# Two of five half swaps of the rotary step: from TensorE matmuls to copies within on-chip memory

## The chip, the cores and the metric

The kernel runs on one core of one Trainium2 chip. The metric is the device time of one execution in microseconds (us); lower is better. The kernel before was measured three times: 1043.47 us in the median, 1043.19 to 1046.55 over the three. On one core five engines work side by side, each on an instruction list of its own: TensorE (PE, matmuls; PEld is its weight load), VectorE (DVE), ScalarE (ACT), GpSimd (POOL) and SyncE (SP, which here only starts the weight transfers). They meet through counting semaphores.

## The reference

The reference is a trunk of two layers on 272 tokens (16 meta tokens and 256 frames) of width 1024. Each layer is a gated feed-forward, a token mixer and a second feed-forward, each between two RMS norms. Layer 0 mixes with stick-breaking attention, layer 1 with grouped-query attention in a sliding window (16 query heads, 4 key heads, head width 64). The change touches layer 1's rotary positions alone:

```python
def rope(t, pos):
    half = HEAD_DIM // 2
    ...
    t1, t2 = tf[..., :half], tf[..., half:]
    return jnp.concatenate([t1 * cos - t2 * sin, t2 * cos + t1 * sin], axis=-1)
```

So each head of queries and keys is its own value times cos, plus its two halves of 32 values swapped, times sin, with a minus on the first half. After it come the scores, the mask, the softmax with sinks, the product with the values and the output projection.

## The kernel before, in words

Activations are kept transposed: a 128-row tile holds two heads (64 rows each) and the tokens lie along the columns. Weights come from HBM in 156 panels of 128 x 2048 float32, 1 MB each. ScalarE rounds a panel half into `w_hi` (L517), VectorE writes what is left into `w_lo` (L765), and TensorE adds three products (w_lo y_hi, w_hi y_hi, w_hi y_lo: L1152 to L1154) for each float32 product. SP starts the load of the panel after next when VectorE has finished both halves of the one that lay in the same buffer (L463).

The attention of layer 1 is written out by hand as a pipeline of slots `st`, in which every engine does the same step of different head pairs. The input projection gives key rows (`b = 0`) and four panels of two query tiles (`b = 1` to `4`). In slot `st` TensorE does one projection tile (`in_tile(st)`, slots 0 to 5; 24 matmuls), then in slots 0, 2, 4, 6 `rotate(b)`, then `scores(st - 1)` (L1397), `values(st - 4)` (L1424), units of the output projection (`out_unit`, 12 matmuls each, from slot 6), and `turn(st - 3)`, which transposes the softmax weights (L1412).

`rotate(b)` (L1370 to L1383) swaps the halves: a float32 matmul of the constant 128 x 128 matrix `rot` with each of the two query tiles, into PSUM bank 5. The minus stands in `rot`. `rope(b)` on VectorE (L971) multiplies that by sin into `rot_s` (L976) and adds `rot_c` (L980), the product with cos, which GpSimd makes (L493). GpSimd does nothing else by then: its loop waits for the query tiles of panel `b` (`sw_drained` at 7 for b = 3, at 9 for b = 4), then makes `rot_c`.

VectorE's order in a slot is: `normalise(st - 3)` (L1002 to L1009), one half of `w_lo` (L765), `drain_tile(st)` (L968, which moves a query tile out of PSUM and raises `sw_drained`), `rope` in slots 2, 4, 6, then `logits(st - 1)` (L993), then `o_low(st - 4)` (L1014), which writes `sw_lo`, an operand of `out_unit`. `rope(3)` stands in slot 4 and `rope(4)` in slot 6; the tile that completes panel 3 is drained in slot 3, the one that completes panel 4 in slot 5. ScalarE's order is `save_p` (L658), a half of `w_hi` (L517), `exps` (L667, L670), then `o_high` (L675), which writes `sw_hi`.

`scores(p)` needs the rotated panel 2 + p//2 and the logits of the pair before; `out_unit(j, n)` needs `sw_lo` of pair 2j + 1.

Of the kernel before, what the change touches and what calls it, by code (L numbers as in the profile page):

```python
# [25 lines left out]
P = 128  # L26
D = 1024
KT = D // P
SEQ = 256
META = 16  # L30
L = META + SEQ
DEPTH = 2
FF = 2816
HD = 64
# [52 lines left out]
SW_K, SW_V, SW_Q = 0, 2, 4  # L87
# [114 lines left out]
def build(nc, first_in, x_in, gains_in, sinks_in, row_in, panels_in, const_in, out):  # L202
    ctx = ExitStack()
    with ctx:
# [3 lines left out]
        def sem(name):  # L208
            return ctx.enter_context(nc.semaphore(name))

        ps = ctx.enter_context(nc.psum_tensor("ps", [P, 8, 512], F32))
# [38 lines left out]
        with ExitStack() as over:  # L250
            first = over.enter_context(nc.sbuf_tensor("first", [P, KT * FIRST_K], F32))
        with ExitStack() as over:
            def mix_sb(name, shape, dt=F32):
                return over.enter_context(nc.sbuf_tensor(name, shape, dt))
            qkv = mix_sb("qkv", [P, 3 * KT, L])
# [8 lines left out]
        with ExitStack() as over:  # L264
            def swa_sb(name, shape, dt=F32):
                return over.enter_context(nc.sbuf_tensor(name, shape, dt))
            swa_sb("under_qkv", [P, 12, L])
            kx = swa_sb("kx", [P, 2, L])
            v_win = swa_sb("v_win", [P, 2, 4, P])
            vt = swa_sb("vt", [P, 4, NKV * HD])  # L270
            rot_s = swa_sb("rot_s", [P, 2, L])
            rot_c = swa_sb("rot_c", [P, 2, 2, L])
            s = swa_sb("s", [P, 3, 2, SW_W])
            p_t = swa_sb("p_t", [P, 2, 2, 512])
            sw_hi = swa_sb("sw_hi", [P, KT, SEQ], F32R)
            sw_lo = swa_sb("sw_lo", [P, KT, SEQ], F32R)
            neg_sinks = swa_sb("neg_sinks", [P, NH])
            neg = swa_sb("neg", [P, 3, 2, 2])
            tot = swa_sb("tot", [P, 3, 2, 2])
            snk = swa_sb("snk", [P, 3, 2, 2])  # L280
            den = swa_sb("den", [P, 3, 2, 2])
            inv = swa_sb("inv", [P, 3, 2, 2])
# [110 lines left out]
        oh_ready = sem("oh_ready")  # L393
        ol_ready = sem("ol_ready")
        rot_done = sem("rot_done")
        rs_ready = sem("rs_ready")
        rc_ready = sem("rc_ready")
        roped = sem("roped")
# [78 lines left out]
        @block.gpsimd  # L477
        def _(pool):

            nc.gpsimd.memset(post_ln[:], 0.0).then_inc(warm_zero, 1)  # L480

            pool.wait_ge(tile_drained, 1)
            for r in range(2):
                nc.gpsimd.memset(w[:, r, :, 0:SB_PAD], 0.0).then_inc(pad_zero, 1)
            pool.wait_ge(const_in_sem, 16)
            for b, at in enumerate((1, 3, 5, 7, 9)):
                pool.wait_ge(sw_drained, at)
                if b >= 2:

                    pool.wait_ge(roped, b - 1)  # L490
                row = SW_K if b == 0 else SW_Q + 2 * b - 2
                c0 = 0 if b == 0 else META
                nc.gpsimd.tensor_tensor(rot_c[:, b % 2, :, c0:L], qkv[:, row:row + 2, c0:L],  # L493
                                        spread(cst("cos"), 2, c0), ALU.mult).then_inc(rc_ready, 1)
                if b == 1:
                    for n, (c, k0, zero) in enumerate(SW_WIN):
                        if zero:
                            nc.gpsimd.memset(v_win[:, :, n, 0:zero], 0.0).then_inc(win_ready, 1)
                        tokens = SW_TOKENS[c][k0 + zero:k0 + P]
                        cut = [i for i in range(len(tokens)) if i == 0 or tokens[i] != tokens[i - 1] + 1] + [len(tokens)]  # L500
                        for i0, i1 in zip(cut, cut[1:]):
                            nc.gpsimd.tensor_copy(v_win[:, :, n, zero + i0:zero + i1],
                                                  qkv[:, SW_V:SW_V + 2, tokens[i0]:tokens[i0] + i1 - i0])\
                                .then_inc(win_ready, 1)
# [254 lines left out]
        def _(v):  # L759
# [68 lines left out]
            for t in SUBS:  # L828
# [121 lines left out]
                elif t.kind == "swa":  # L950
# [20 lines left out]
                    def rope(b):  # L971
                        c0 = 0 if b == 0 else META
                        row = SW_K if b == 0 else SW_Q + 2 * b - 2
                        turned = ps[:, 0:2, 0:L] if b == 0 else ps[:, 5, :].rearrange("p (a n) -> p a n", a=2)
                        v.wait_ge(rot_done, b + 1)
                        nc.vector.tensor_tensor(rot_s[:, :, c0:L], turned, spread(cst("sin"), 2, c0),  # L976
                                                ALU.mult).then_inc(rs_ready, 1)
                        v.wait_ge(rs_ready, b + 1)
                        v.wait_ge(rc_ready, b + 1)
                        nc.vector.tensor_tensor(qkv[:, row:row + 2, c0:L], rot_s[:, :, c0:L],  # L980
                                                rot_c[:, b % 2, :, c0:L], ALU.add).then_inc(roped, 1)
                        v.wait_ge(roped, b + 1)
# [165 lines left out]
        def _(pe):  # L1148
# [8 lines left out]
            for t in SUBS:  # L1157
# [197 lines left out]
                elif t.kind == "swa":  # L1355
# [83 lines left out]
                    def out_unit(j, n):  # L1439

                        g = t.g_out + j
                        pe.wait_ge(lo_ready, 2 * g + 2)
                        pe.wait_ge(ol_ready, 8 + 2 * j + 2)
                        if j == 0 and n < 2:
                            pe.wait_ge(sw_drained, 8 + n)
                        elif j == 0 and n == 2:
                            pe.wait_ge(rs_ready, 5)
                        elif j == 0:
                            pe.wait_ge(neg_ready, 4 * PAIRS)
                        for d in (2 * n, 2 * n + 1):  # L1450
                            for c in range(2):
                                opens = j == c == 0 and (d % 2 == 0 or n == 3)
                                mm = three(out_tile(ps, t, d), g % SLOTS, D * c + P * d, sw_hi[:, 2 * j + c, :],
                                           sw_lo[:, 2 * j + c, :], opens, j == 3 and c == 1, shared=n < 3)
                            if j == 3:
                                mm.then_inc(f_done, 1)
                        if j < 3 and n == 3:
                            mm.then_inc(panel_done, 1)

                    pe.wait_ge(const_in_sem, 16)  # L1460
                    for st in range(SW_SLOTS):
                        if st < SW_TILES:
                            in_tile(st)
                        for unit in SW_FILL.get(st, ([], []))[0]:
                            out_unit(*unit)
                        if st == 0:
                            rotate(0)
                            rotate(1)
                        elif st in (2, 4, 6):
                            rotate(st // 2 + 1)  # L1470
                        if 0 <= st - 1 < PAIRS:
                            scores(st - 1)
                        if st == 1:
                            turn_v()
                        if 0 <= st - 4 < PAIRS:
                            values(st - 4)
                        for unit in SW_FILL.get(st, ([], []))[1]:
                            out_unit(*unit)
                        if 0 <= st - 3 < PAIRS:
                            turn(st - 3)  # L1480
# [106 lines left out]
def constants():  # L1587

    c = np.zeros((P, CONST_W), np.float32)

    def part(name):
        lo, hi = CONST[name]
        return c[:, lo:hi]

    p = np.arange(P)
    for n in range(3):
        q = np.arange(SB_Q0[n], L)
        key = SB_KEY[n] + p
        seen = (key[:, None] < q[None, :]) & (key[:, None] >= (256 if n == 2 else 0))
        part("mask_sb")[:, SB_COL[n]:SB_COL[n] + len(q)] = np.where(seen, 0, HIDDEN)  # L1600
    part("tri")[:] = p[:, None] >= p[None, :]
    part("ident")[:] = np.eye(P)
    part("ones")[:] = 1
    for n in range(2):
        key = np.array(SW_TOKENS[n])
        key_chunk = np.where(key < META, -1, (key - META) // CHUNK)
        own = (2 * n + p // CHUNK)[:, None]
        seen = (key_chunk == -1) | ((key_chunk >= own - 1) & (key_chunk <= own))
        part("mask_sw")[:, SW_COL[n]:SW_COL[n] + len(key)] = np.where(seen, 0, HIDDEN)
    first = p % HD < HD // 2  # L1610
    part("rot")[np.where(first, p + HD // 2, p - HD // 2), p] = np.where(first, -1, 1)
    freq = np.float32(THETA) ** (-np.arange(HD // 2, dtype=np.float32) / np.float32(HD // 2))
    angle = np.arange(L, dtype=np.float32)[None, :] * freq[p % (HD // 2)][:, None]
    part("cos")[:] = np.cos(angle)
    part("sin")[:] = np.sin(angle)
    return c


# [64 lines left out]
```

## Time and profile before

| | |
|---|---|
| median of 3 runs | 1043.47 us |
| the profiled execution: its own time | 1043.83 us |
| its span | 1042.0 us |
| TensorE busy | 1028.1 us (99%) |
| VectorE busy | 642.7 us (62%) |
| ScalarE busy | 518.9 us (50%) |
| GpSimd busy | 10.5 us (1%) |
| mean granted TensorE clock | 0.999 of full speed |

Span is from the first to the last profiled instruction; the execution's own time holds 1.83 us more. Busy shares are means over the whole kernel; the attention slots that the change touches lie between about 775 and 844 us.

### The profile page before, as it was taken

What the parts mean: (1) busy time and instruction counts of PE and PEld (TensorE: products, weight loads), DVE (VectorE), ACT (ScalarE), POOL (GpSimd) and SP (SyncE); (2) the same over time, 40 slices, a digit from 0 to 9 for tenths busy, and PEclk for the clock granted to TensorE, in tenths of its full rate; (3) what the DMA queues carried; (4) which work ended last, traced back from release to release, by engine and by line L of the source; (5) the groups of instructions that cost most, each with busy time, mean ns of one, the idle gap of its engine ahead of it and who ended that gap; (6) DMA issues with size and microseconds to landing.
All of it is one profiled execution on the core that took longest, in us unless ns stands there. A gap on an engine that the chain in (4) does not pass through costs nothing.

```text
span 1042.0 us, 19997 instructions
## 1 busy us (share of the span) xinstructions
PE 1028.1 (99%) x8070; PEld 996.9 (96%) x8070; DVE 642.7 (62%) x896; ACT 518.9 (50%) x742; POOL 10.5 (1%) x19
## 2 busy tenths in 40 slices
PE   9999999999999999999999999999999999999997
PEld 8999999999999999999999999999998999999886
DVE  6765553478775866555447755544588777765532
ACT  5643443446665564434345544343457755544433
POOL 0000000000000000000000000000021000000000
PEclk9999999999999999999999999999999999999999
DMA  8665554514343256455442654455413335655451
GB/s 326 208 236 166 183 176 165 186 53 154 131 137 110 78 207 237 161 168 192 165 168 75 242 190 172 164 183 178 162 42 122 116 129 203 219 184 194 170 182 40
DMA packets 24534, 171.26 MB, mean 164 GB/s; under 512 B 2977, under 2 KB 2977, under 8 KB 4385
## 3 DMA queue, kind: packets, MB, share of 16 engines
q1 hardware_dynamic: 24048, 169.49, 46.6%
q8 instruction: 41, 0.67, 0.3%
q10 hardware_dynamic: 432, 1.00, 0.2%
q14 instruction: 13, 0.10, 0.0%
HBM read 169.43 MB, written 1.05 MB: 164 GB/s over the span
## 4 chain that ended last, share of the span: by engine, by line
PE 87%; DVE 5%; DMA 3%; ACT 3%; issue 1%; SPq 0%; DVEq 0%; ACTq 0%
PE ps L1152 24%; PE ps L1154 24%; PE ps L1153 23%; DMA raw<-in_panels_dram 3%; PE ps L1491 2%; PE ps L1492 2%; PE ps L1490 2%; PE ps L1188 2%; PE ps L1197 2%; PE ps L1190 2%; DVE w_lo L765 1%; ACT w_hi L517 1%; PE ps L1257 1%; PE ps L1312 1%; PE ps L1412 1%
## 5 line engine op out<-in xcount | busy, mean ns | idle before, releaser
L517 ACT CAST w_hi<-raw 128x1024 fp32r<-128x1024 f32 x312 | 312.5, 1047 | 401.6 <-PE ps L1154 295.7
L765 DVE TENSOR_TENSOR w_lo<-raw,w_hi 128x1024 fp32r<-128x1024 f32 x312 | 370.0, 1225 | 193.8 <-ACT w_hi L517 193.4
L1152 PE MATMUL ps<-y_hi,w_lo 128*128 128x272 f32 (+1 forms) x1458 | 421.8, 289 | 0.9 <-DVE pre_ms L794 0.8
L1154 PE MATMUL ps<-y_lo,w_hi 128*128 128x272 f32 (+1 forms) x1458 | 418.9, 287 | 0.0
L1153 PE MATMUL ps<-y_hi,w_hi 128*128 128x272 f32 (+1 forms) x1458 | 417.3, 286 | 0.0
L1152 PEld LDWEIGHTS ps<-y_hi,w_lo 128*128 128x128 f32 x1458 | 274.7, 188 | 3.1 <-DVE w_lo L765 1.2
L1153 PEld LDWEIGHTS ps<-y_hi,w_hi 128*128 128x128 f32 x1458 | 274.6, 188 | 0.2
L1154 PEld LDWEIGHTS ps<-y_lo,w_hi 128*128 128x128 f32 x1458 | 274.7, 188 | 0.0
L1152 PE MATMUL ps<-h_hi,w_lo 128*128 (+1 forms) x528 | 152.1, 288 | 0.0
L1153 PE MATMUL ps<-h_hi,w_hi 128*128 (+1 forms) x528 | 152.0, 288 | 0.0
L1154 PE MATMUL ps<-h_lo,w_hi 128*128 (+1 forms) x528 | 151.2, 286 | 0.0
L1152 PEld LDWEIGHTS ps<-h_hi,w_lo 128*128 128x128 f32 x528 | 99.4, 188 | 0.0
L1153 PEld LDWEIGHTS ps<-h_hi,w_hi 128*128 128x128 f32 x528 | 99.4, 188 | 0.0
L1154 PEld LDWEIGHTS ps<-h_lo,w_hi 128*128 128x128 f32 x528 | 99.3, 188 | 0.0
L843 DVE TENSOR_TENSOR hid<-act,ps 128x544 f32<-128x544 f32 (+1 forms) x44 | 31.2, 710 | 70.2 <-PE ps L1154 70.2
L838 DVE TENSOR_TENSOR act<-ps,rms_inv 128x544 f32<-128x544 f32 (+1 forms) x44 | 31.5, 716 | 55.1 <-PE ps L1154 51.4
L1188 PE MATMUL ps<-y_hi,w_lo 128*128 128x272 f32 (+1 forms) x238 | 61.9, 292 | 3.6 <-DVE y_hi L1114 2.8
L1190 PE MATMUL ps<-y_hi,w_hi 128*128 128x272 f32 (+1 forms) x238 | 60.5, 286 | 0.0
L1188 PEld LDWEIGHTS ps<-y_hi,w_lo 128*128 128x128 f32 x238 | 44.8, 188 | 7.0 <-DVE y_hi L1114 4.9
L1190 PEld LDWEIGHTS ps<-y_hi,w_hi 128*128 128x128 f32 x238 | 44.8, 188 | 0.0
L1197 PE MATMUL ps<-y_lo,w_hi 128*128 128x272 f32 (+1 forms) x238 | 36.3, 286 | 0.0
L531 ACT ACTIVATE y_hi<-xT,gains 128x272 fp32r<-128x272 f32 (+1 forms) x35 | 18.2, 521 | 34.7 <-DVE xT L1136 34.7
(173 smaller groups left out, 1034.2 us busy)
## 6 DMA issues: line engine op xcount, KB each, us to landing
raw<-in_panels_dram SPq DMA_DIRECT2D x156, 1024.0 KB, 4.9
first<-in_first_dram SPq DMA_DIRECT2D x3, 784.0 KB, 7.0
xT<-in_x_dram SPq DMA_DIRECT2D x1, 1088.0 KB, 13.6
out_dram<-fT SPq DMA_DIRECT2D x4, 256.0 KB, 2.0
const<-in_const_dram ACTq DMA_DIRECT2D x1, 920.0 KB, 10.0
first<-in_first_dram SPq DMA_DIRECT2D x2, 392.0 KB, 3.6
gain_row<-in_row_dram SPq DMA_DIRECT2D x1, 512.0 KB, 5.6
gains<-in_gains_dram ACTq DMA_DIRECT2D x1, 48.0 KB, 3.5
```

The costliest lines, as they stand in the source:

```text
L517: nc.scalar.copy(w_hi[:, g % SLOTS, part], raw_part(g, part)).then_inc(hi_ready, 1)
L765: nc.vector.tensor_tensor(w_lo[:, g % SLOTS, part], raw_part(g, part), w_hi[:, g % SLOTS, part].bitcast(F32), ALU.subtract).then_inc(lo_re ...
L838: nc.vector.tensor_tensor(act[:, j % 2, :, t0:L], ps[:, b0:b0 + 2, t0:L], spread(rms_inv, 2, t0), ALU.mult).then_inc(gate_ready, 1)
L843: nc.vector.tensor_tensor(hid[:, j % 2, :, t0:L], act[:, j % 2, :, t0:L], ps[:, b0:b0 + 2, t0:L], ALU.mult).then_inc(h_ready, 1)
L1152: nc.tensor.matmul(dst, w_lo[:, slot, pc], yh, start=first, stop=False, skip_group_check=shared)
L1153: nc.tensor.matmul(dst, w_hi[:, slot, pc], yh, start=False, stop=False, skip_group_check=shared)
L1154: return nc.tensor.matmul(dst, w_hi[:, slot, pc], yl, start=False, stop=last, skip_group_check=shared)
L1188: nc.tensor.matmul(dst, w_lo[:, g % SLOTS, pc], y_hi[:, k, c0:L], start=(k == 0), stop=False)
L1190: nc.tensor.matmul(dst, w_hi[:, g % SLOTS, pc], y_hi[:, k, c0:L], start=False, stop=False)
L1197: nc.tensor.matmul(ps[:, BANK_IN[i][c], c0:L], w_hi[:, g % SLOTS, pc], y_lo[:, k, c0:L], start=False, stop=False)
L1490: nc.tensor.matmul(dst, hh[:, cols], w_lo[:, slot, at:at + 512], start=first, stop=False)
L1491: nc.tensor.matmul(dst, hh[:, cols], w_hi[:, slot, at:at + 512], start=False, stop=False)
```

## The change

The panels b = 3 and b = 4 no longer go through `rotate`. GpSimd copies their halves by four transfers each within on-chip memory, 32 partitions x 2 tiles x 256 columns of float32 (64 KB) each, into a new buffer `swapped`. For b = 4 it first waits until VectorE has read the buffer for b = 3. VectorE waits for all four transfers and reads `swapped` where it read PSUM. The minus moves from the matrix `rot` to the table `sin`. The unit `out_unit(0, 2)`, which writes the PSUM bank that `rotate` used, waits for `rope(2)` and no longer for `rope(4)`.

```diff
+            swapped = swa_sb("swapped", [P, 2, SEQ])
...
+            def swap_halves(pool, b):
+                row = SW_Q + 2 * b - 2
+                if b >= 4:
+                    pool.wait_ge(rs_ready, b)
+                for at in range(0, P, HD // 2):
+                    src = at ^ (HD // 2)
+                    pool.dma_start(swapped[at:at + HD // 2], qkv[src:src + HD // 2, row:row + 2, META:L])\
+                        .then_inc(swap_landed, 16)
+
             for b, at in enumerate((1, 3, 5, 7, 9)):
                 pool.wait_ge(sw_drained, at)
+                if b >= 3:
+                    swap_halves(pool, b)
                 if b >= 2:
                     pool.wait_ge(roped, b - 1)
...
-                        turned = ps[:, 0:2, 0:L] if b == 0 else ps[:, 5, :].rearrange("p (a n) -> p a n", a=2)
-                        v.wait_ge(rot_done, b + 1)
+                        if b < 3:
+                            v.wait_ge(rot_done, b + 1)
+                            turned = ps[:, 0:2, 0:L] if b == 0 else ps[:, 5, :].rearrange("p (a n) -> p a n", a=2)
+                        else:
+                            v.wait_ge(swap_landed, 64 * (b - 2))
+                            turned = swapped[:]
...
                         elif j == 0 and n == 2:
-                            pe.wait_ge(rs_ready, 5)
+                            pe.wait_ge(rs_ready, 3)
...
-                        elif st in (2, 4, 6):
-                            rotate(st // 2 + 1)
+                        elif st == 2:
+                            rotate(2)
...
-    part("rot")[np.where(first, p + HD // 2, p - HD // 2), p] = np.where(first, -1, 1)
+    part("rot")[np.where(first, p + HD // 2, p - HD // 2), p] = 1
...
-    part("sin")[:] = np.sin(angle)
+    part("sin")[:] = np.where(first, -1, 1)[:, None] * np.sin(angle)
```

## Rows read from the trace of the kernel before

**Rows 1.** Page, engines: busy time, share of the span, instructions.

```profile
span 1042.0 us, 19997 instructions
PE 1028.1 (99%) x8070; PEld 996.9 (96%) x8070; DVE 642.7 (62%) x896; ACT 518.9 (50%) x742; POOL 10.5 (1%) x19
```

**Rows 2.** Windows: length, busy time (instructions) by engine, PE clock, DMA share, GB/s.

```profile
795.00:805.00 10.00, 10.00 (x104) 8.64 (x102) 9.80 (x35) 7.52 (x27) 1.27 (x1) 1.00 0.32 107
805.00:815.00 10.00, 10.00 (x98) 8.75 (x98) 8.18 (x29) 7.46 (x23) 0.00 (x0) 1.00 0.31 107
```

**Rows 3.** Chain that ended last: start, length, what. Attention slots 6, 7 and the end.

```profile
806.82 0.86 PE ps L1380 x4
...
811.32 0.87 PE ps L1412 x8
...
831.17 2.28 DVE w_lo L765 x2
833.61 4.95 DMA raw<-in_panels_dram
838.59 2.00 ACT w_hi L517 x2
```

**Rows 4.** Timeline, TensorE: start, length, line, count; the rotations and what follows.

```profile
795.15 0.28 PE L1154 MATMUL ps<-y_lo,w_hi 128*128 128x256 f32 x1
795.27 1.02 PE L1380 MATMUL ps<-qkv,const 128*128 128x256 f32 x4
796.23 0.39 PE L1397 MATMUL ps<-kx,qkv 64*128 64x144 f32 x1
...
805.14 0.36 PE L1152 MATMUL ps<-sw_hi,w_lo 128*128 128x256 f32 x1
```

**Rows 5.** Timeline, VectorE: in brackets idle time before and who ended it.

```profile
790.50 0.17 DVE L1002 TENSOR_TENSOR den<-tot,snk 128x4 f32<-128x4 f32 x1 [1.90 <-ACT snk L670]
...
795.00 0.97 DVE L1009 TENSOR_SCALAR s<-s,inv 128x144 f32<-128x144 f32 x4
...
797.37 0.68 DVE L976 TENSOR_TENSOR rot_s<-ps,const 128x512 f32<-128x512 f32 x1
798.08 0.69 DVE L980 TENSOR_TENSOR qkv<-rot_s,rot_c 128x512 f32<-128x512 f32 x1
...
804.61 0.42 DVE L1014 TENSOR_TENSOR sw_lo<-ps,sw_hi 128x256 fp32r<-128x256 f32 x1
...
806.24 1.22 DVE L765 TENSOR_TENSOR w_lo<-raw,w_hi 128x1024 fp32r<-128x1024 f32 x1
807.72 0.69 DVE L976 TENSOR_TENSOR rot_s<-ps,const 128x512 f32<-128x512 f32 x1 [0.26 <-PE ps L1380]
...
814.66 0.37 DVE L993 CUSTOM_DVE_ANT_0 s<-ps,const,neg_sinks 128x144 f32<-128x144 f32 x1 [1.35 <-PE ps L1397]
```

**Rows 6.** Timeline, GpSimd: its products for panels 3 and 4.

```profile
793.43 1.30 POOL L493 TENSOR_TENSOR rot_c<-qkv,const 128x512 f32<-128x512 f32 x1 [9.57 <-DVE qkv L968]
803.36 1.27 POOL L493 TENSOR_TENSOR rot_c<-qkv,const 128x512 f32<-128x512 f32 x1 [8.62 <-DVE qkv L968]
```

**Rows 7.** Page, DMA issues: count, KB each, median us from issue to landing.

```profile
out_dram<-fT SPq DMA_DIRECT2D x4, 256.0 KB, 2.0
gains<-in_gains_dram ACTq DMA_DIRECT2D x1, 48.0 KB, 3.5
```

**Rows 8.** Timeline, SP's queue: start and length of single issues.

```profile
3.10 0.49 SPq L455 DMA_DIRECT2D raw<-in_panels_dram  x1
...
797.29 0.33 SPq L463 DMA_DIRECT2D raw<-in_panels_dram  x1
...
807.65 0.33 SPq L463 DMA_DIRECT2D raw<-in_panels_dram  x1
```

**Rows 9.** Timeline, ScalarE, after the turns of pairs 3 and 6.

```profile
811.79 1.07 ACT L658 COPY p_t<-ps 128x512 f32<-128x512 f32 x2 [1.68 <-PE ps L1412]
...
827.45 1.08 ACT L658 COPY p_t<-ps 128x512 f32<-128x512 f32 x2 [0.57 <-PE ps L1412]
```

More of the change, by code:

```diff
@@ L395, in build @@
         rot_done = sem("rot_done")
+        swap_landed = sem("swap_landed")
         rs_ready = sem("rs_ready")
```

## The prediction, made before the result was known

> **What bounds the kernel now.** I read the page's engine line first: TensorE is busy 1028.1 us of a span of 1042.0 [rows 1], so a matmul taken away from a stretch in which TensorE never waits is worth its full length, if nothing else is as late as TensorE there. The windows of the attention slots come next: from 795 to 815 us TensorE is busy throughout, but in the first ten of these VectorE is busy 9.80 us as well [rows 2]. So there are two candidates, and the question is which one carries the order of things. The chain of waits runs through TensorE in slots 6 and 7 and has `rotate(4)` on it [rows 3]. VectorE's timeline shows the other half of the truth: after its wait that ended at 790.50 it has no gap worth a bracket until `rope(4)`, which waited 0.26 us for TensorE [rows 5]. In these 17 us VectorE sets its own pace and TensorE sets its own, and both arrive together: TensorE starts `out_unit(0, 0)` at 805.14 [rows 4], and the `sw_lo` that this unit needs comes from VectorE's instruction of 804.61, which ends at 805.03 [rows 5]. The reader is to see there that TensorE has only about 0.1 us of room to be early at that point.
>
> After 807 VectorE waits again (1.35 us before the logits of slot 7, for the scores) [rows 5], and ScalarE waits for TensorE's turns (1.68 and 0.57 us) [rows 9]. From there all engines hang on TensorE, and the last load before the stage's end, issued at 833.61, hangs on them in turn: `w_lo` at 831.17 releases it, and ScalarE's casts at 838.59 wait for it [rows 3]. What TensorE has gained or lost by slot 7 is therefore carried to the end of the layer.
>
> **What is removed.** Two rotations, each four matmul records (two float32 matmuls). `rotate(3)` starts at 795.27 and the scores behind it at 796.23, that is 0.96 us [rows 4]; the same step in the chain, with overlaps taken off, is 0.86 us for `rotate(4)` [rows 3]. I take 0.87 for each, 1.74 us together. That is the most that the change can give.
>
> `rotate(3)` is worth little: TensorE would arrive at `out_unit(0, 0)` 0.87 us earlier and find `sw_lo` not there before 805.03 plus a semaphore's passage, about 805.05. Gain 0.1 us, the rest turns into a wait. `rotate(4)` lies behind that point and is worth its 0.87. Without any new wait the sum is -0.1 - 0.87 = -1.0 us.
>
> **What is added: eight transfers, issued by GpSimd, and a wait of VectorE for them.** GpSimd begins panel 3 at 793.43 and panel 4 at 803.36, as it now begins `rot_c` [rows 6]. VectorE wants the swapped halves at 797.37 (panel 3) [rows 5], and for panel 4 when its `w_lo` half of 806.24 ends, 807.46 [rows 5]. The room is 797.37 - 793.43 = 3.94 us and 807.46 - 803.36 = 4.10 us. Let S be the time from GpSimd's start to the landing of the fourth transfer. VectorE then waits X3 = S - 3.94 and X4 = S - 4.10, or nothing if these are negative.
>
> No row shows a transfer issued by GpSimd, nor one within on-chip memory, so S is bounded. From below: three issues at the length of SP's short ones, 0.33 us [rows 8], then the shortest landing on the page, 2.0 us for the output of 256 KB in four [rows 7]: S = 3.0. From above: each issue as long as a GpSimd instruction on these tiles, 1.30 us [rows 6], and the landing of the 48 KB `gains` at the start, 3.5 us [rows 7]: S = 3 x 1.30 + 3.5 = 7.4. My value: the issue of a panel load at the start, 0.49 us [rows 8], times the ratio in which GpSimd is slower than VectorE on the same shape, 1.30 to 0.69 [rows 5, 6], is 0.93 us; three of them, and the landing of 2.0 made longer by the slower issue (0.93 - 0.49 = 0.44): S = 2.8 + 2.44 = 5.2. The nearest rows are the issue and the small landing, which is why I stay below the middle of a range whose top borrows the loaded start of the kernel. The bytes are small (64 KB a transfer), though the weight loads of 797.29 and 807.65 [rows 8] run against the last of them.
>
> With S = 5.2: X3 = 1.3 and X4 = 1.1 us. Behind VectorE's wait in slot 4 are queued the add of `rope(3)`, the logits of pair 3, `sw_lo` of pair 0, the normalising of pairs 2 and 3, a `w_lo` half, two more drains and `sw_lo` of pair 1. TensorE waits for that last one: it has no room, as shown, so X3 is paid in full, and `out_unit(0, 0)` starts at 805.05 + 1.3. X4 is paid in part. Behind `rope(4)` the first thing that TensorE needs is again a logits step and a `sw_lo`; VectorE idled 1.35 us before the logits of slot 7, of which 0.26 more are freed since it no longer waits for `rotate(4)`, and 1.0 us is used up because TensorE's scores come that much earlier: room 1.35 + 0.26 - 1.0 = 0.6 us. So X4 costs 1.1 - 0.6 = 0.5 us. Sum: -1.0 + 1.3 + 0.5 = +0.8 us.
>
> The formula that the range uses: change = -1.0 + X3 + max(0, X4 - 0.6). It crosses zero at S = 4.8.
>
> **A rule against the change.** In the two windows VectorE runs four TENSOR_SCALAR steps of `normalise`, 0.97 us together at 795.00 in the first [rows 5]. The Trainium skill, page "SBUF — State Buffer", section "Who interferes with whom", has it that a transfer issued from GpSimd gets no descriptors while VectorE is in a two-port mode, which tensor_scalar can enter. No row here shows it. What it would do here is rival (c) below.
>
> By the Trainium skill, page "DMA: Bandwidth & Descriptors", section "Anatomy of one DMA — SWDGE (gpsimd) path", a GpSimd transfer has a fixed 2.0 us, mostly the landing's receipt, and making descriptors costs little; then four together would be nearer the lower bound, and the change that of rival (a). No row shows that either.
>
> **What costs nothing.** `rot_c` moves behind the four issues: 793.43 + 4 x 0.93 = 797.15, plus 1.30 is 798.45, while the add needs it at 798.08 before and at 799.4 with X3 = 1.3 [rows 5, 6]. The same in slot 6. If the landing were quick but the issues slow, 0.4 us of it would show. The sin product reads on-chip memory in place of PSUM: 0.68 us against the 0.69 of the add, which reads on-chip memory alone [rows 5]. The buffer's reuse waits for the product of 797.37, long over at 803.36. The earlier wait of `out_unit(0, 2)` frees nothing: it starts behind the turn of 811.32 [rows 3], when `rope(4)` of 807.72 [rows 5] is done. The moved minus changes no instruction.
>
> **The rivals.**
> (a) Hidden. S below 3.94: no new wait, and the change is -1.0 us. For it: SP's issues of 0.33 and landings of 2.0. Against it: the slow GpSimd, four issues in a row on one queue.
> (b) Slower, beyond what a measurement overlooks. Place: GpSimd's queue between the drain of a panel's second tile and `rope`. Price: with 1.30 us an issue and 2.9 us or more for the landing, S = 6.8 to 7.4; at 7.1, X3 = 3.2, X4 = 3.0, sum -1.0 + 3.2 + 2.4 = +4.6 us. It decides from S = 6.4 on, where the sum passes +3.1. A first transfer of GpSimd's that is dearer than the rest would fall on X3, which has no room at all.
> (c) GpSimd's issues are held off while VectorE runs the four TENSOR_SCALAR steps, 0.97 us in each window [rows 5]: S = 5.2 + 0.97 = 6.2, X3 = 2.3, X4 = 2.1, sum -1.0 + 2.3 + 1.5 = +2.8 us.
> (d) VectorE is not as tight as I read it, and `rotate(3)` pays in full too: -1.74 us, with S small. Against it: the 9.80 of 10 us [rows 2].
>
> **How the numbers follow.** The profiled execution took 1043.83 us (1.83 more than its span), 0.36 above the median of 1043.47; a difference found on it is put onto the median. Chances: forecast (S 4.3 to 5.8, change -0.6 to +2.0) 0.41; (a) 0.23; (b) 0.20; (c) 0.08; (d) 0.04; something that I don't see and that makes it faster, 0.04. Time: 1043.5 + 0.8 = 1044.3 us. The range begins at rival (a) with a little for the spread of medians, 1042.2, and ends at 1048.0, which is (b) at its middle; the upper half of (b) and part of (d) are left out. What a measurement of this kernel can tell from no change is about 0.3%, 3.1 us: all of the forecast, (a), (d) and (c) are inside, (b) is outside. That gives same 0.76 and slower 0.20. Faster by 3.1 us is more than the two rotations hold, hence 0.04.
>
> **What would show it.** Right: no L1380 at 795 and 806, the four L1380 records of slot 2 left, GpSimd's eight issues from 793.4 and 803.4, and VectorE's L976 of slots 4 and 6 with idle time of 1.3 and 1.1 us before them, ended by the swap; `out_unit(0, 0)` at about 806.3, the load that before was issued at 833.61 at about 834.4. Wrong: no idle time at L976 (rival a), over 2 us of it (b, c), or TensorE ahead of 805 at `out_unit(0, 0)` (d). The prediction fails outright if the granted clock falls in the new waits, or if a transfer from GpSimd costs time outside the attention slots.

## The result, and the profile after

The changed kernel takes 1046.41 us in the median of 20 executions, the kernel before 1044.59 us in 20 on the same chip: a ratio of 1.0026, 95% interval [1.0015, 1.0038], or +2.7 us (1.6 to 4.0). This ratio, like the others below, is not the quotient of the two medians, which lie 1.8 us apart (1.0017). The forecast was +0.8 us, in the class of no change within 0.3%. The time lies in the range and in the class, but it is over three times as far above before as forecast (over twice by the medians), and the loss does not come by the way that the prediction gave. The profiled execution of after took 1047.46 us, with a span of 1045.7 (before 1043.83 and 1042.0).

The page of after: engines [rows 1], the queue that is new (packets, MB, share of the DMA engines), and the transfers' landing (count, KB each, median us).

```profile
span 1045.7 us, 19986 instructions
...
PE 1028.7 (98%) x8062; PEld 997.8 (95%) x8062; DVE 646.7 (62%) x896; ACT 519.3 (50%) x742; POOL 15.0 (1%) x27
...
q0 software_dynamic: 256, 0.52, 0.2%
...
swapped<-qkv POOLq DMA_DIRECT2D x8, 64.0 KB, 1.9
```

VectorE has as many instructions as before, 896, and is busy 4.0 us longer. A change that gives VectorE nothing more to do has made something on it slower. The windows of after (as [rows 2], with the window at 845 beside them):

```profile
795.00:805.00 10.00, 9.13 (x98) 7.85 (x96) 9.86 (x27) 7.53 (x27) 1.81 (x3) 1.00 0.36 120
805.00:815.00 10.00, 8.82 (x90) 7.96 (x92) 9.79 (x32) 6.73 (x22) 3.21 (x5) 1.00 0.42 133
845.00:850.00 5.00, 3.00 (x13) 3.03 (x14) 3.32 (x8) 2.84 (x11) 0.00 (x0) 0.68 0.62 210
```

TensorE is no longer full (9.13 and 8.82 of 10), VectorE is (9.86 and 9.79). The timeline of after says with what. GpSimd:

```profile
793.00 2.29 POOL L495 DMA_DIRECT2D swapped<-qkv  x4 [8.56 <-DVE qkv L982]
795.30 1.28 POOL L507 TENSOR_TENSOR rot_c<-qkv,const 128x512 f32<-128x512 f32 x1
804.76 2.15 POOL L495 DMA_DIRECT2D swapped<-qkv  x4 [8.17 <-DVE qkv L982]
806.93 1.30 POOL L507 TENSOR_TENSOR rot_c<-qkv,const 128x512 f32<-128x512 f32 x1
```

VectorE (as [rows 5]; the row of 794.30 with x2 and the row of 806.39 with x1 are the first instructions of the groups shown below them):

```profile
790.25 0.97 DVE L1027 TENSOR_SCALAR s<-s,inv 128x144 f32<-128x144 f32 x4
...
794.30 2.42 DVE L1027 TENSOR_SCALAR s<-s,inv 128x144 f32<-128x144 f32 x2
794.30 2.87 DVE L1027 TENSOR_SCALAR s<-s,inv 128x144 f32<-128x144 f32 x4
...
798.55 0.68 DVE L994 TENSOR_TENSOR rot_s<-swapped,const 128x512 f32<-128x512 f32 x1
...
802.02 0.97 DVE L1027 TENSOR_SCALAR s<-s,inv 128x144 f32<-128x144 f32 x4
...
806.39 1.93 DVE L1027 TENSOR_SCALAR s<-s,inv 128x144 f32<-128x144 f32 x1
806.39 2.61 DVE L1027 TENSOR_SCALAR s<-s,inv 128x144 f32<-128x144 f32 x4
...
810.07 0.68 DVE L994 TENSOR_TENSOR rot_s<-swapped,const 128x512 f32<-128x512 f32 x1
```

Two things are to be seen. The products of the swapped tiles (L994) have no bracket: nobody waits for a transfer. And the group of four TENSOR_SCALAR steps (L1027, the L1009 of before) takes 0.97 us twice, and 2.87 and 2.61 us in the two places where `rot_c` runs beside it; in the second of these one instruction alone takes 1.93. TensorE, which now waits where it had been just in time [rows 4], and later at the first sums of squares:

```profile
806.18 0.36 PE L1170 MATMUL ps<-sw_hi,w_lo 128*128 128x256 f32 x1 [1.56 <-issue]
...
847.00 0.76 PE L1573 MATMUL ps<-sq,const 128*128 128x128 f32 x2 [2.40 <-ACT sq L754]
```

The second wait begins in the chain that ended last, with a load (before: 4.95 us [rows 3]):

```profile
831.83 2.28 DVE w_lo L779 x2
...
834.27 6.89 DMA raw<-in_panels_dram
...
841.19 2.00 ACT w_hi L531 x2
```

The row of the kernel before that answers to 847.00 had waited 0.46 us:

```profile
844.40 0.46 PE L1555 MATMUL ps<-sq,const 128*128 128x128 f32 x2 [0.46 <-ACT sq L740]
```

So there are two losses, apart in place and kind: a stretch of VectorE in slots 4 and 6, and a load that lands 1.9 us later, with TensorE's granted clock at 0.68 in the window that holds the end of the wait of 2.40: a mean of stretches at 2.4 and at 1.2 GHz. The pair of matmuls behind the wait takes 0.76 us there, and 0.46 in before. A window of 1 us shows the lower level by itself (PEclk 0.50, that is 1.2 GHz; before has 1.00 there):

```profile
847.00:848.00 1.00, 1.00 (x5) 1.00 (x6) 1.00 (x3) 0.20 (x2) 0.00 (x0) 0.50 0.93 393
```

### The profile page after: what moved, and what is told of

The parts are those of the page before. It is cut to its first block, busy times and chain, and to the rows that moved or that the text cites. A ratio compares the mean times of both kernels' runs of the same rounds, so it can differ in the third digit from the quotient of the medians.

```text
span 1045.7 us, 19986 instructions
## 1 busy us (share of the span) xinstructions
PE 1028.7 (98%) x8062; PEld 997.8 (95%) x8062; DVE 646.7 (62%) x896; ACT 519.3 (50%) x742; POOL 15.0 (1%) x27
## 4 chain that ended last, share of the span: by engine, by line
PE 87%; DVE 7%; ACT 3%; DMA 2%; issue 1%; DVEq 0%; POOL 0%; SPq 0%; ACTq 0%; POOLq 0%
PE ps L1170 24%; PE ps L1171 23%; PE ps L1172 23%; PE ps L1206 2%; PE ps L1208 2%; PE ps L1215 2%; PE ps L1509 2%; PE ps L1510 2%; PE ps L1508 2%; DMA raw<-in_panels_dram 2%; DVE w_lo L779 1%; PE ps L1275 1%; ACT w_hi L531 1%; PE ps L1330 1%; DVE s L1027 1%
```

## The experiments

Three numbers of each trace carry the argument. **Slots**: from the first TENSOR_SCALAR group (790.91 before, 790.25 after) to the issue of the last load (833.61, 834.27), with before's 42.70 taken off. **Landing** of that load. **Rest**: span less the load's issue, so all that follows. These three come from one profiled execution a kernel (two each for before and after). The timed ratio is to the kernel before on the same chip, with its 95% interval; the kernels were not all timed on one chip.

| kernel | slots | landing | rest | timed ratio |
|---|---|---|---|---|
| before | 0 | 4.95 | 208.4 | |
| before again | -0.03 | 4.9 | 208.3 | |
| product late (before) | +0.82 | 5.1 | 208.7 | 1.0013 [1.0004, 1.0023] |
| extra transfers (before) | +0.34 | 4.9 | 208.3 | 0.9991 [0.9980, 1.0003] |
| after | +1.32 | 6.9 | 211.4 | 1.0026 [1.0015, 1.0038] |
| after again | +1.33 | 7.7 | 212.0 | |
| cos first | +0.29 | 5.9 | 209.4 | 1.0016 [1.0006, 1.0026] |
| swap on SP | -0.30 | 6.4 | 209.9 | 1.0012 [1.0003, 1.0021] |
| last panel only | -0.37 | 7.8 | 212.8 | 1.0014 [1.0002, 1.0026] |
| no swap | -1.01 | 6.9 | 211.2 | 0.9994 [0.9981, 1.0007] |
| after, padded | +1.33 | 5.2 | 208.5 | 1.0005 [0.9995, 1.0015] |
| no swap, padded | -0.86 | 4.9 | 208.3 | 0.9988 [0.9978, 0.9997] |
| swap on SP, padded | -0.13 | 5.0 | 208.4 | 0.9997 [0.9988, 1.0006] |
| last on SP, padded | -0.71 | 5.1 | 208.5 | 0.9996 [0.9985, 1.0006] |

The rest grows for two reasons. With landings of 5.9 and 6.4 us (cos first, swap on SP) it is longer by as much as the landing, 1.0 and 1.5, and the granted clock is 1.00 from 840 to 860 us. With landings of 6.9 to 7.8 (after twice, last panel only, no swap) it is 0.9 to 1.5 us longer than the landing explains, and in all four TensorE's granted clock is 0.50 for three or more whole microseconds between 846 and 853.

**The product late.** The kernel before, with `rot_c` held back until it stands beside the TENSOR_SCALAR steps; no transfer, all rotations kept.

```diff
+                if b >= 3:
+                    pool.wait_ge(inv_ready, 2 * b - 4)
```

> The kernel before, with GpSimd's cos products for panels 3 and 4 held back until VectorE has its reciprocal of the same slot, so that they start just as VectorE's four TENSOR_SCALAR steps start. No transfer is issued by GpSimd. Theory 1 (a running GpSimd tensor product locks VectorE's TENSOR_SCALAR out, and that is what stretched it from 0.97 to 2.87 and 2.61 us after the change): both groups of four stretch by 1.2 us or so, to about 2.2 us, and the time rises by about 1 us, since the first delay is paid in full and the second disappears in VectorE's 1.35 us of idle time in slot 7. Theory 2 (it is the issuing of transfers by GpSimd that locks VectorE out): 0.97 us as before, and no change of the time.

Timeline, VectorE and GpSimd:

```profile
793.87 2.00 DVE L1011 TENSOR_SCALAR s<-s,inv 128x144 f32<-128x144 f32 x4
794.01 1.30 POOL L495 TENSOR_TENSOR rot_c<-qkv,const 128x512 f32<-128x512 f32 x1 [10.24 <-DVE inv L1006]
...
805.11 2.01 DVE L1011 TENSOR_SCALAR s<-s,inv 128x144 f32<-128x144 f32 x4
805.25 1.31 POOL L495 TENSOR_TENSOR rot_c<-qkv,const 128x512 f32<-128x512 f32 x1 [9.94 <-DVE inv L1006]
```

The median was 1044.09 us (11 executions) beside 1043.53 (35). The product alone, put beside the steps, makes 0.97 into 2.00 and 2.01, with no transfer anywhere, and costs 0.82 us in the slots. That shows that the product by itself makes such a stretch. It is 1.03 long here and 1.90 and 1.64 in after; the excess is not explained by the product's recorded time, and its cause stays open.

**Cos first.** After, with the four issues put behind `rot_c`.

```diff
-                if b >= 3:
-                    swap_halves(pool, b)
...
+                if b >= 3:
+                    swap_halves(pool, b)
```

> The changed kernel, with the cos product of panels 3 and 4 made before the four transfers are issued, so that the issues (about 2.2 us) run beside VectorE's TENSOR_SCALAR steps and the product doesn't. Theory 1 (the product locks): the four steps take 0.97 us as before the change; the swaps land 1.3 us later, so VectorE waits about 1.0 us before the sin product of panel 3 and 0.8 us before that of panel 4; in all about +0.2 us against the kernel before. Theory 2 (the issues lock): the steps take 2.5 to 3 us again, and the time is 2 us or more above the kernel before.

```profile
792.42 1.29 POOL L505 TENSOR_TENSOR rot_c<-qkv,const 128x512 f32<-128x512 f32 x1 [8.48 <-DVE qkv L982]
793.65 2.32 POOL L495 DMA_DIRECT2D swapped<-qkv  x4
...
793.99 1.02 DVE L1027 TENSOR_SCALAR s<-s,inv 128x144 f32<-128x144 f32 x4
...
797.66 0.69 DVE L994 TENSOR_TENSOR rot_s<-swapped,const 128x512 f32<-128x512 f32 x1 [1.19 <-DMA swapped<-qkv]
...
808.37 0.69 DVE L994 TENSOR_TENSOR rot_s<-swapped,const 128x512 f32<-128x512 f32 x1 [0.64 <-DMA swapped<-qkv]
```

The timeline shows issues right beside the TENSOR_SCALAR steps, which stay at 1.02 (1.08 in slot 6). The stretch is gone, so the issues alone do not make it, and now the wait that the prediction had in mind is there, 1.19 and 0.64 us. The slots come out at +0.29, that is 1.3 us above the -1.0 without a wait (below): the 1.19 and a little more. The median was 1044.93 (12), so it did not get back below before: the landing was 5.9.

**Swap on SP.** After, with the same eight transfers issued from SP's queue, between the weight loads; GpSimd as before the change.

```diff
+            load(122, 0)
+            swap_halves(3)
+            load(123, 0)
+            swap_halves(4)
+            load(124, 0)
```

> The changed kernel, with the eight transfers issued from SP's queue, between the weight loads that it issues at about 785, 797 and 808 us, and GpSimd left with its cos products at their old time. Both theories: TENSOR_SCALAR at 0.97 us, the transfers landed within 4 x 0.33 + 2 = 3.3 us, before VectorE asks, no wait at the sin product, and the removed rotations show: -1.0 us against the kernel before. Rival: on SP's queue a weight load is held back by the wait for the drained tiles, and the time doesn't fall.

```profile
797.11 0.69 DVE L1001 TENSOR_TENSOR rot_s<-swapped,const 128x512 f32<-128x512 f32 x1 [0.62 <-DMA swapped<-qkv]
...
806.99 0.69 DVE L1001 TENSOR_TENSOR rot_s<-swapped,const 128x512 f32<-128x512 f32 x1
```

TENSOR_SCALAR stays at 0.98, one wait of 0.62 is left, the slots gain 0.30. The median is 1044.62 (11), above before all the same: landing 6.4, rest +1.5. With neither stretch nor GpSimd transfers a loss remains, and it lies behind the slots.

**Last panel only.** After, with `rotate(3)` put back; only panel 4 goes by transfer (the waits that count panels are moved with it).

```diff
-                if b >= 3:
+                if b >= 4:
                     swap_halves(pool, b)
...
-                        elif st == 2:
-                            rotate(2)
+                        elif st in (2, 4):
+                            rotate(st // 2 + 1)
```

> The changed kernel, with the swap by transfer for panel 4 alone; panel 3 goes through TensorE as before. Theory 1 and 2: the first TENSOR_SCALAR group is 0.97 us again, the second 2.6 us; TensorE saves 0.87 us and the stretch of 1.64 us meets 0.74 us of VectorE's idle time (1.35 + 0.26 - 0.87), so it costs 0.9 us: 0.0 us against the kernel before. If the two panels' costs don't act in this order, the time stands between that of the changed kernel and this.

```profile
795.00 0.98 DVE L1027 TENSOR_SCALAR s<-s,inv 128x144 f32<-128x144 f32 x4
...
803.59 2.30 POOL L495 DMA_DIRECT2D swapped<-qkv  x4 [8.86 <-DVE qkv L982]
...
805.33 2.65 DVE L1027 TENSOR_SCALAR s<-s,inv 128x144 f32<-128x144 f32 x4
805.90 1.30 POOL L507 TENSOR_TENSOR rot_c<-qkv,const 128x512 f32<-128x512 f32 x1
```

The stretch follows the panel: 0.98 in slot 4, 2.65 in slot 6. It costs 0.5 us there (-0.37 against the 0.87 of the rotation gained), so most of it is absorbed. The median is 1045.62 (12), 2.1 us above before and not level with it as expected; the profiled execution, the slowest of the twelve, has a landing of 7.8 and a rest 4.4 us longer.

**Extra transfers.** The kernel before, with eight transfers of the same size issued by GpSimd behind `rot_c`. They copy a piece of a constant, and nobody reads the copy; VectorE waits for them only at the end of the stage.

```diff
+                if b >= 3:
...
+                    for at in range(0, P, HD // 2):
...
+                        pool.dma_start(swapped[at:at + HD // 2], const[src:src + HD // 2, 0:2 * L]
...
+                            .then_inc(swap_landed, 16)
```

> The kernel before, with all its rotations on TensorE, and eight extra transfers of the same shape from GpSimd behind the cos products of panels 3 and 4, whose result nobody reads. What is open is why the variant with transfers from SP's queue, which is ahead of the kernel before by 1.2 us when it issues the last weight load of the attention slots, is not faster at the end: that load landed after 6.4 us there, 5.9 to 7.8 in the other three kernels with swap transfers, and 5.0 and 5.1 in the two without. Theory L (the transfers on the queues make that later load slow): 6 us or more here too, and the time 1 to 2 us above the kernel before. Theory M (taking the rotations out moves the load into a worse moment): 5.0 us here, and the time within 0.3 us of the kernel before. TENSOR_SCALAR at 0.97 us in both.

TENSOR_SCALAR took 1.00 and 1.12 us beside the issues, the landing of the last load was 4.9, the median 1043.21 (12) beside 1043.55 (23). The slots are 0.34 us longer in the trace, but the transfers themselves cost nothing that the timing shows. They stand where cos first has them; no run had them issued ahead of the product and unread.

**No swap.** After, without transfers and without a wait; the product with sin reads the unswapped tiles, so the swap of panels 3 and 4 is left out of the computation.

```diff
-                            v.wait_ge(swap_landed, 64 * (b - 2))
-                            turned = swapped[:]
+                            turned = qkv[:, row:row + 2, META:L]
```

> The changed kernel without its eight transfers and without a wait for them: the sin product of panels 3 and 4 reads the unswapped tiles, so the swap of these panels is left out of the computation. It measures what two rotations on TensorE are worth. By the prediction's step: out_unit(0, 0) 0.1 us earlier, everything from slot 7 on 1.0 us earlier, the time -1.0 us. Theory L: the last load lands in 5.0 us and the 1.0 us is kept to the end. Theory M: the load takes 6 us or more and the time is that of the kernel before or above it.

```profile
804.99 0.36 PE L1157 MATMUL ps<-sw_hi,w_lo 128*128 128x256 f32 x1 [0.65 <-issue]
```

The slots gain 1.01 us. `out_unit(0, 0)` stands 14.09 us behind the first group (804.99 - 790.90), against 14.23 before (805.14 - 790.91): TensorE arrived early and waited 0.65, as the prediction had it for `rotate(3)`. Yet the timing is 0.9994 (1043.77, 12 executions), since the landing is 6.9 and the rest +2.8 us. In this trace the load is late with neither a transfer nor a changed GpSimd, with only the rotations missing.

**After again, before again.** One execution each, unchanged, for the scatter of the landing.

> The changed kernel once more, for one look. If the late landing of the last load (6.9 us) belongs to the kernel, it shows again within 0.5 us; if it is a matter of the single execution, it lies anywhere between 4.8 and 8. The TENSOR_SCALAR groups are 2.9 and 2.6 us again in both cases.

> The kernel before once more, for one look: the last load at 5.0 us again if its landing belongs to the kernel; the load issued at 781, which took 6.1 us in the first profile and 4.9 to 5.9 in the others, tells how far one load's time scatters between executions.

```profile
834.80 7.67 DMA raw<-in_panels_dram
```

That is after, with 1048.62 us; before again took 1043.10, landing 4.9. The slots repeat to 0.03 us; the landing scatters by more than the 0.5 us expected (6.9 and 7.7) but stays on its side of 5.2. Other loads of these stretches land late too, in kernels with all rotations: the one issued at 781 took 6.1 us in before, the one issued at 818 took 6.2 in before again. So what goes with the missing rotations is that this load is late, the one on the chain; it is so in 6 of 6 traces without them and in 0 of the 4 with them.

**Padded kernels.** What all kernels with a late load share is a shorter list of matmuls in slots 4 or 6. So each missing rotation is replaced by two matmuls of one column, written to an unused bank; they are as many matmul records (8070 as in before) and nearly no work.

```diff
+                        elif st in (4, 6):
+                            pe.wait_ge(sw_drained, st + 3)
+                            pe.wait_ge(rs_ready, 3)
+                            for _ in range(2):
+                                nc.tensor.matmul(ps[0:1, 5, 0:1], const[:, 0:1], const[:, 0:1], start=True, stop=True,
+                                                 skip_group_check=True)
```

The swap on SP with it:

> The variant with the transfers issued from SP's queue, with two float32 matmuls of one column put in slots 4 and 6 where the rotations stood, so that TensorE's instruction list is as long as in the kernel before up to that place and behind it (they write one element of an unused bank). In all six executions in which rotations were missing, the last load of the attention slots landed 5.9 to 7.8 us after its issue, in all four with every rotation present after 4.9 to 5.1. Theory M1 (what makes the load late is where TensorE's instruction list is cut into the 16 KB packets in which it is fetched): the load lands in 5.0 us again, and the time is about 0.7 us below the kernel before (1.0 less the short matmuls and the 0.6 us of waiting for the swap). Theory M2 (the load is late since it is issued at another moment): 6 us or more again, and the time 1 us above the kernel before.

No swap with it (the swap of panels 3 and 4 is left out here too):

> The kernel without rotations and without transfers for panels 3 and 4 (the swap of these panels is left out of the computation), with the same four short matmuls. M1: load 5.0 us, time 0.7 to 0.9 us below the kernel before: the worth of the two rotations as the prediction had it. M2: load 6 us or more, the time that of the unpadded variant.

After with it:

> The changed kernel with the same four short matmuls. M1: the load lands in 5.0 us and the time is that of the changed kernel less 2 us: about 1.2 us above the kernel before, which is what the two locked-out stretches cost net of the rotations. M2: nothing changes against the changed kernel. The TENSOR_SCALAR groups stay at 2.9 and 2.6 us.

The padded after, timeline and chain:

```profile
793.78 2.88 DVE L1027 TENSOR_SCALAR s<-s,inv 128x144 f32<-128x144 f32 x4
...
807.26 0.24 PE L1493 MATMUL ps<-const 128*1 128x1 f32 x4
```

```profile
833.76 5.15 DMA raw<-in_panels_dram
```

In all three the landing is back at 4.9 to 5.2 and the rest at 208.3 to 208.5, while the slots keep what they had within 0.17 us (+1.33 for after, stretch and all). The timed ratios fall with it: after 1.0026 to 1.0005, swap on SP 1.0012 to 0.9997, no swap 0.9994 to 0.9988. Of these falls only that of after is about as large as the intervals are wide; those of the other two lie within them, and the kernels of each pair were timed in separate sets, each beside its own executions of before. The medians were 1044.07, 1043.81 and 1042.75 (12 each) beside 1043.63 (29).

Why fewer matmuls make a load late is not settled. One companion in the trace can be followed: TensorE's instruction list is itself fetched, in packets of 16 KB. In 770 to 850 us the queue that carries it has (packets, MB, share), in before, and then in after:

```profile
q8 instruction: 6, 0.10, 0.5%
```

```profile
q8 instruction: 5, 0.08, 0.4%
```

It is 6 in every trace with a landing of 4.9 to 5.2 us (in no swap, padded, whose trace lies 3 us later, in 773 to 853), and 5 in every one with a later landing. But the packet that makes the difference comes behind the load, and so cannot be what delays it: it starts between 848 and 850 in before and between 854 and 856 in after, where the load had landed at 841.2, and in each of the six late traces it starts over 10 us after the landing. The packet before it starts between 832 and 838 beside the load, within 1 us of its issue, in the early traces and in the late ones alike. So the places at which the list is cut do move with the padding, but no fetch of that list was found that only the late loads meet, and the cause stays open. In the late landings most DMA engines are done early: in after 0.06 of the DMA engines' time is busy from 839 to 840 and 0.07 from 840 to 841, about one engine of 16, and all wait for that remnant.

**Last on SP, padded.** The version that the experiments point to: `rotate(3)`, worth 0.1 us, stays on TensorE; panel 4 is swapped from SP's queue; two small matmuls stand in slot 6. The lines are shown against the padded swap on SP.

```diff
             load(122, 0)
-            swap_halves(3)
             load(123, 0)
             swap_halves(4)
...
-                        if b < 3:
+                        if b < 4:
```

> Of panels 3 and 4 only panel 4 is swapped by transfers, issued on SP's queue; panel 3 goes through TensorE as before, and the slot of panel 4's missing products holds two one-column float32 matmuls. Theory (the lock-out of VectorE's TENSOR_SCALAR steps by the late rot_c, and the late landing of the last load where TensorE's instructions are fewer): neither is there. TENSOR_SCALAR groups of panels 3 and 4 at 0.97 us, the last load at 5.0 us, one rotation (0.87 us) less and the small matmuls (0.12 us by half of the 0.24 us group) more: 0.75 us under the kernel before, ratio 0.9993. Rival: the kernel with both panels on SP's queue (ratio 0.9997) lost nothing at panel 3, so nothing is gained by giving panel 3 back, and this one comes out at 0.9997 or above; or the instruction list is cut otherwise again, the last load takes 6 us or more, and the ratio is 1.001 or above.

```profile
794.49 0.97 DVE L1031 TENSOR_SCALAR s<-s,inv 128x144 f32<-128x144 f32 x4
...
802.79 2.62 SPq L472 DMA_DIRECT2D swapped<-qkv  x4
...
804.85 0.98 DVE L1031 TENSOR_SCALAR s<-s,inv 128x144 f32<-128x144 f32 x4
...
806.88 0.69 DVE L998 TENSOR_TENSOR rot_s<-swapped,const 128x512 f32<-128x512 f32 x1
```

In the trace each step is as expected: no stretch, no wait, slots -0.71, landing 5.1. The median is 1042.84 (11) beside 1043.47 (15), ratio 0.9996, with an interval [0.9985, 1.0006] that holds the 0.9993 expected and holds 1 too. It beats after; that it beats before is not shown.

## Why the prediction was right in its class, and by another way

**The gain: right.** -1.0 without a wait, of which `rotate(3)` 0.1 and `rotate(4)` 0.87. No swap gives -1.01 in the slots, -0.86 with the small matmuls, and in time 0.9988, or -1.25 us (-2.3 to -0.3). Reading VectorE's gapless 17 us [rows 5] beside TensorE's 99% [rows 1] was the step that carried this; rival (d), -1.74, is out.

**The cost of the transfers: wrong, S = 5.2.** An issue took 0.54 to 0.57 us (2.29 and 2.15 for four), not 0.93, and the landing 1.9, not 2.44. Three issues and a landing are 3.6 us, inside the room of 3.94 and 4.10, and the waits X3 = 1.3 and X4 = 1.1 are absent. Both came out too high through one assumption, that GpSimd issues as much more slowly as it computes [rows 5, 6]. Taken alone, rival (a) had this right. The Trainium skill, page "DMA: Bandwidth & Descriptors", section "Anatomy of one DMA — SWDGE (gpsimd) path", which the prediction quoted for it, gives such a transfer a fixed 2.0 us, near the 1.9 measured.

**"`rot_c` moves behind the four issues ... What costs nothing": the step that failed.** It asked when the product is needed, and not what it would run beside. It runs beside the TENSOR_SCALAR steps, which stop there: +1.90 and +1.64 us, of which the late product shows 1.03 to be the product's own doing. That is a stretch on VectorE in both slots where the prediction had a wait, and of nearly its size; so the rest of the working held. The first is paid almost in full (`out_unit(0, 0)` stands 15.93 us behind the first group, 1.70 later than in before and 1.84 later than in no swap), the second for 0.5 of 1.64 (by last panel only): more room than the 0.6 that I counted. -1.0 + 1.84 + 0.5 is +1.34, and +1.32 was measured. The nearness of the forecast is chance: two terms wrong in opposite directions.

**Rival (c) had the resource and the wrong victim.** It let GpSimd's issues wait for VectorE. Issues beside the steps took 2.15 to 2.32 us for four wherever they stood and stretched the steps by 0.03 to 0.15; it was VectorE that stopped, for the product. The Trainium skill, page "SBUF — State Buffer", section "Who interferes with whom", has the lock in both directions, by order of issue, with the other engine fully blocked. After agrees that VectorE can be the one that stops, 1.93 us for one step of a group that takes 0.97 for four; the order of issue is not borne out by the recorded starts, since that step began at 806.39, 0.54 us before the product's recorded start. The trace of before had shown it too, and I passed over it. VectorE's timeline there has a `w_lo` of 2.27 us, beside 1.22 [rows 5]:

```profile
774.33 2.27 DVE L765 TENSOR_TENSOR w_lo<-raw,w_hi 128x1024 fp32r<-128x1024 f32 x1
```

and GpSimd's timeline has products up to 775.45:

```profile
772.89 2.62 POOL L493 TENSOR_TENSOR rot_c<-qkv,const 128x544 f32<-128x544 f32 x2 [542.61 <-DVE qkv L960]
```

**What no part of the prediction had: the late load.** It had the load's issue at 834.4 (it was 834.27), and then took the rest as fixed. A landing of 6.9 and a rest of +3.0 us weigh more than the +1.32 of the slots. In time the parts are: no swap padded to after padded, the stretch, +1.8 us (0.9988 to 1.0005, in one set); after padded to after, the load, +2.2 us (to 1.0026, in another set); with -1.25 that is +2.7. By my estimate from the intervals each of the two steps is uncertain by about 1.5 us; the medians give +1.3 and +1.4. "The prediction fails outright if the granted clock falls in the new waits" came near: it fell to 0.68, though behind the wait for the load and not in the slots, where the same window of before has 1.00, and about 1.1 of the +3.0 us is left for it when the landing's 1.9 is taken off:

```profile
845.00:850.00 5.00, 4.43 (x32) 3.78 (x31) 3.94 (x13) 1.58 (x5) 0.00 (x0) 1.00 0.31 129
```

## What to carry to other kernels

When a step moves on an engine, look at what the two engines beside it run in its new place, not only at when its result is wanted; a row of the same operation with two durations in the trace of before is the place where such a lock already shows. Work of 1.3 us on an engine that is 1% busy went with a stretch of 1.9 us on the one that sets the pace. And where a change shortens an instruction list, a kernel whose list is padded to the old length is a cheap comparison: here it took back a late landing that the change's own traffic could have been blamed for.

## What the runs showed that I had not expected

- VectorE's TENSOR_SCALAR on float32 in on-chip memory stops for a GpSimd product with on-chip operands: four steps take 2.00 us in place of 0.97 when the product starts 0.14 us behind the first, 2.60 to 2.88 when the product follows four DMA issues. In after the step that stopped in slot 4 began by 794.6, about 0.7 us before the product's recorded start of 795.30.
- A GpSimd issue of a 64 KB copy took 0.54 to 0.58 us and landed in 1.9; on SP's queue the same took 0.63 to 0.66 (2.51 to 2.63 for four) against 0.33 for a 1 MB load [rows 8].
- Two groups of four matmul records of one column, 0.24 us a group, stood between a landing of 6.89 and of 5.15 us of a 1 MB load issued some 27 us behind the second; in the other two pairs of kernels the landing went from 6.9 to 4.9 and from 6.4 to 5.0.
